# Two of the four sums of Strassen's weight blocks made by accumulating DMAs of GpSimd's queue, with signs of the combinations turned

## What is computed

```
h = rmsnorm(concat(meta_tokens, x), norm_gain)
q, k, v, f_logit, z_att, u, gate_b, gate_c, z_conv, m_att, m_conv = split(h @ w_in)
y_att  = (forgetting_attention(q, k, v, log_sigmoid(f_logit + b_f)) * silu(z_att)) @ w_att_o
y_conv = (gate_b * short_conv(gate_c * u, conv_w) * silu(z_conv)) @ w_conv_o
out    = rmsnorm(x + (sigmoid(m_att) * y_att + sigmoid(m_conv) * y_conv) @ w_out, final_gain)
```

## Time and profile before

| what | us |
|---|---|
| median of 3 runs | 1209.1 |
| lowest, highest | 1209.03, 1209.93 |
| the profiled execution, first to last instruction | 1207.9 |
| PE busy | 1196.4 (99%) |
| DVE busy | 954.6 (79%) |
| ACT busy | 651.3 (54%) |
| POOL busy | 35.3 (3%) |
| PE idle in 40 to 600 us, by the windows | 2.1 |
| DVE busy in 40 to 600 us | 518.7 of 560 |

### The profile page before, as it was taken

One profiled execution on the slowest core, in us unless ns is written; L12 is line 12 of the kernel. 1 busy time (PEld: TensorE's weight loads), 2 busy tenths in 40 slices (PEclk: granted clock), 3 DMA queues, 4 the chain that ended last, 5 costly groups with the idle time before them and its releaser, 6 DMA issues.

```text
span 1207.9 us, 18441 instructions
## 1 busy us (share of the span) xinstructions
PE 1196.4 (99%) x7252; PEld 1070.4 (89%) x7252; DVE 954.6 (79%) x1111; ACT 651.3 (54%) x868; POOL 35.3 (3%) x50
## 2 busy tenths in 40 slices
PE   9999999999999999999999999999999999999997
PEld 8998898898888988889888899999999999888886
DVE  6989988988989989999966556877787778755544
ACT  7666555556656566656555444445544554543533
POOL 1000000000000000000000010111011101000000
PEclk9999999999999999999999999999999999999999
DMA  6788898887888898898578865555655565665663
GB/s 214 241 296 274 272 296 262 276 301 257 273 288 288 272 293 287 268 310 271 192 234 267 268 188 179 157 168 163 210 155 173 154 200 169 219 212 176 213 221 123
DMA packets 181249, 280.40 MB, mean 232 GB/s; under 512 B 9296, under 2 KB 128160, under 8 KB 180768
## 3 DMA queue, kind: packets, MB, share of 16 engines
q1 hardware_dynamic: 171760, 263.49, 66.9%
q10 hardware_dynamic: 9408, 15.78, 4.2%
HBM read 270.83 MB, written 8.41 MB: 231 GB/s over the span
## 4 chain that ended last, share of the span: by engine, by line
PE 87%; DVE 10%; issue 1%; ACT 1%; DMA 0%; ACTq 0%; POOLq 0%; POOL 0%; DVEq 0%
PE ps L1481 22%; PE ps L1483 22%; PE ps L1482 22%; PE ps L1497 7%; PE ps L1496 6%; PE ps L1498 3%; PE ps L1495 3%; DVE w_lo L1052 2%; DVE w_lo L1089 2%; DVE w_lo L1086 2%; DVE quads L1068 1%; DVE quads L1070 1%; DVE quads L1066 1%; DMA chan_rows<-in_norm_gain 0%; PE ps L1506 0%
## 5 line engine op out<-in xcount | busy, mean ns | idle before, releaser
L934 DVE TENSOR_TENSOR w_lo<-w_raw,w_hi 128x1024 fp32r<-128x1024 f32 x196 | 238.6, 1235 | 97.9 <-ACT w_hi L610 96.9
L1481 PE MATMUL ps<-h,w_hi 128*128 128x258 f32 (+1 forms) x1024 | 293.6, 287 | 1.3 <-DVE w_lo L1052 1.0
L1482 PE MATMUL ps<-h,w_hi 128*128 128x258 f32 (+1 forms) x1024 | 291.2, 284 | 0.0
L1483 PE MATMUL ps<-h,w_lo 128*128 128x258 f32 (+1 forms) x1024 | 291.0, 284 | 0.0
L610 ACT CAST w_hi<-w_raw 128x1024 fp32r<-128x1024 f32 x198 | 203.8, 1050 | 112.0 <-PE ps L1483 64.2
L1481 PEld LDWEIGHTS ps<-h,w_hi 128*128 128x128 f32 x1024 | 192.7, 188 | 5.3 <-issue 1.8
L1482 PEld LDWEIGHTS ps<-h,w_hi 128*128 128x128 f32 x1024 | 192.9, 188 | 2.1
L1483 PEld LDWEIGHTS ps<-h,w_lo 128*128 128x128 f32 x1024 | 192.8, 188 | 0.0
L1052 DVE TENSOR_TENSOR w_lo<-w_raw,w_hi 128x1024 fp32r<-128x1024 f32 x122 | 148.7, 1220 | 15.9 <-ACT w_hi L666 15.7
L1497 PE MATMUL ps<-h,w_hi 128*128 128x512 f32 x408 | 159.9, 397 | 1.0 <-DVE w_lo L1052 0.9
L1496 PE MATMUL ps<-h,w_hi 128*128 128x512 f32 x360 | 142.5, 396 | 0.0
(11 more groups left out here) (213 smaller groups left out, 2085.9 us busy)
## 6 DMA issues: line engine op xcount, KB each, us to landing
w_raw<-in_w_in SPq DMA_DIRECT2D x226, 512.0 KB, 4.8
quads<-in_w_in SPq DMA_DIRECT2D x144, 512.0 KB, 4.3
w_raw<-in_w_conv_o SPq DMA_DIRECT2D x32, 512.0 KB, 5.8
w_raw<-in_w_att_o SPq DMA_DIRECT2D x32, 512.0 KB, 4.5
w_raw<-in_w_out SPq DMA_DIRECT2D x32, 512.0 KB, 4.3
quads<-in_w_in SPq DMA_DIRECT2D x48, 256.0 KB, 4.7
gates_dram<-stage ACTq DMA_DIRECT2D x24, 256.0 KB, 4.5
gate_nat<-gates_dram ACTq DMA_DIRECT2D x8, 512.0 KB, 4.5
```

The costliest lines, as they stand in the source:

```text
L934: nc.vector.tensor_tensor(w_lo[:, lo_slot(c), :], w_raw[:, c % RAW, :], w_hi[:, hi_slot(c), :].bitcast(F32), ALU.subtract).then_inc(w_spli ...
L1481: nc.tensor.matmul(dst, a_hi, b_hi, start=start, stop=False, skip_group_check=resumed)
L1482: nc.tensor.matmul(dst, a_hi, b_lo, start=False, stop=False, skip_group_check=resumed)
L1483: return nc.tensor.matmul(dst, a_lo, b_hi, start=False, stop=stop, skip_group_check=resumed)
```

## The change

The right half of row 0 of a quad, b12, gets its first sum from a DMA. GpSimd waits until the two loads of the buffer have landed (`quad_landed`) and issues a DMA of 128 by 512 floats (256 KB) from `w_in` that is added to what lies there (`accum_op=ALU.add`). In a first-half step it adds b11, in a second-half step b22, both read from HBM again. The end of this DMA is told by three new semaphores `t_added`, one for each buffer. 96 such DMAs stand in GpSimd's list, ahead of its loop for the attention stage.

DVE no longer does anything for the first-half sum, and does two sums instead of three in a second-half step. ACT's cast of the first-half sum waits for `t_added`, and so does DVE's first sum of a second-half step. The loads on SP's queue are unchanged: all four blocks are still loaded, b22 for its own product.

Since a DMA can add and not subtract, b12 now enters as b12 + b11 and b12 + b22, that is with the sign of the right block column turned. This is made good elsewhere: a sum of the frame blocks becomes a difference (line 1115 of the kernel before), and two sums of frame blocks and two of the four output blocks of each group are made by SCALAR_TENSOR_TENSOR, -1 times the first operand minus the second. These 14 instructions replace 14 TENSOR_TENSOR of the same size.

The cut diff:

```diff
     found = []
     for step, after in enumerate(STEP_AFTER):
         before = STEP_AFTER[step - 1] if step > 0 else -3
-        if step < STEPS:
-            places = [(after, 0)]
-        else:
-            spread = min(3, after - before)
-            places = [(after - spread + 1 + part * spread // 3, part) for part in range(3)]
-        found += [(g, step, part) for place, part in places if place == r]
+        if step >= STEPS:
+            spread = min(2, after - before)
+            places = [(after - spread + 1 + part * spread // 2, part) for part in range(2)]
+            found += [(g, step, part) for place, part in places if place == r]
     return found
...
-    per = STEPS + 3 * STEPS
-    return g * per + (step + 1 if step < STEPS else STEPS + 3 * (step - STEPS) + part + 1)
+    return (g * STEPS + step - STEPS) * 2 + part + 1
...
+        t_added = [sem(f"t_added{q}") for q in range(QUADS)]
...
+        def quad_added(g, step):
+            return ((g * len(STEP_AFTER) + step) // QUADS + 1) * 16
...
+
+            w_in_k = w_in.rearrange("(k p) n -> p k n", p=P)
+            for g in range(GROUPS):
+                for step in range(2 * STEPS):
+                    q, k = quad(g, step), 2 * (step % STEPS) + step // STEPS
+                    col = quad_col(g) + k % 2 * HALF
+                    pool.wait_ge(quad_landed[q], quad_fill(g, step))
+                    nc.gpsimd.dma_start(quads[:, q, 0, HALF:], w_in_k[:, k, col:col + HALF], accum_op=ALU.add
+                                        ).then_inc(t_added[q], 16)
+
             with pool.Fori(0, PAIRS) as i:
...
-                    act.wait_ge(t_made, sums_made(g, step, 0))
+                    act.wait_ge(t_added[q], quad_added(g, step))
                     act.wait_ge(w_used, slot_reused(c + 1))
                     nc.scalar.copy(w_hi[:, hi_slot(c + 1), 0:HALF], quads[:, q, 0, HALF:]).then_inc(w_rounded, 1)
                 else:
-                    act.wait_ge(t_made, sums_made(g, step, 1))
+                    act.wait_ge(t_made, sums_made(g, step, 0))
                     act.wait_ge(w_used, slot_reused(c))
                     nc.scalar.copy(w_hi[:, hi_slot(c), :], quads[:, q, 0, :]).then_inc(w_rounded, 1)
-                    act.wait_ge(t_made, sums_made(g, step, 2))
+                    act.wait_ge(t_made, sums_made(g, step, 1))
                     act.wait_ge(w_used, slot_reused(c + 1))
                     nc.scalar.copy(w_hi[:, hi_slot(c + 1), :], quads[:, q, 1, :]).then_inc(w_rounded, 1)
...
                 q = quad(g, step)
-                b11, b12, b21, b22 = (quads[:, q, k, n * HALF:(n + 1) * HALF] for k in range(2) for n in range(2))
+                b11, b12, b21 = (quads[:, q, k, n * HALF:(n + 1) * HALF] for k, n in ((0, 0), (0, 1), (1, 0)))
                 if part == 0:
-                    dve.wait_ge(quad_landed[q], quad_fill(g, step))
-                else:
-                    dve.wait_ge(t_made, sums_made(g, step, part - 1))
-                if step < STEPS:
-                    nc.vector.tensor_tensor(b12, b12, b11, ALU.subtract).then_inc(t_made, 1)
-                elif part == 0:
-                    nc.vector.tensor_tensor(b12, b22, b12, ALU.subtract).then_inc(t_made, 1)
-                elif part == 1:
+                    dve.wait_ge(t_added[q], quad_added(g, step))
                     nc.vector.tensor_tensor(b11, b12, b11, ALU.add).then_inc(t_made, 1)
                 else:
-                    nc.vector.tensor_tensor(b21, b11, b21, ALU.subtract).then_inc(t_made, 1)
+                    dve.wait_ge(t_made, sums_made(g, step, 0))
+                    nc.vector.tensor_tensor(b21, b11, b21, ALU.add).then_inc(t_made, 1)
...
                 elif n == 7:
                     dve.wait_ge(s_step, 2)
-                    nc.vector.tensor_tensor(a22, a21, a22, ALU.add).then_inc(s_made, 1)
+                    nc.vector.tensor_tensor(a22, a22, a21, ALU.subtract).then_inc(s_made, 1)
...
                 elif n == 12:
-                    nc.vector.tensor_tensor(a11, a22, a11, ALU.subtract).then_inc(s_made, 1)
+                    nc.vector.scalar_tensor_tensor(out=a11, in0=a22, scalar=-1.0, in1=a11, op0=ALU.mult,
+                                                   op1=ALU.subtract).then_inc(s_made, 1)
                 elif n == 13:
                     dve.wait_ge(s_made, 3)
                     dve.wait_ge(s_step, 4)
-                    nc.vector.tensor_tensor(a12, a12, a11, ALU.subtract).then_inc(s_made, 1)
+                    nc.vector.scalar_tensor_tensor(out=a12, in0=a12, scalar=-1.0, in1=a11, op0=ALU.mult,
+                                                   op1=ALU.subtract).then_inc(s_made, 1)
...
-                    nc.vector.tensor_tensor(stage[1][:], stage[2][:], ps[:, P5_BANK, :], ALU.add
-                                            ).then_inc(c12_made, 1)
+                    nc.vector.scalar_tensor_tensor(out=stage[1][:], in0=stage[2][:], scalar=-1.0,
+                                                   in1=ps[:, P5_BANK, :], op0=ALU.mult, op1=ALU.subtract
+                                                   ).then_inc(c12_made, 1)
                     dve.wait_ge(c12_made, g + 1)
                     nc.vector.tensor_tensor(stage[2][:], stage[2][:], ps[:, P7_BANK, :], ALU.add
                                             ).then_inc(v_made, 1)
                     dve.wait_ge(v_made, g + 1)
                     dve.wait_ge(gate_stored[C11], (g + 1) * 16)
-                    nc.vector.tensor_tensor(stage[0][:], stage[2][:], ps[:, P2_BANK, :], ALU.subtract
+                    nc.vector.tensor_tensor(stage[0][:], stage[2][:], ps[:, P2_BANK, :], ALU.add
                                             ).then_inc(c21_made, 1)
                     dve.wait_ge(c21_made, g + 1)
                     dve.wait_ge(p5_kept, g + 1)
-                    nc.vector.tensor_tensor(stage[2][:], stage[2][:], p5[:], ALU.add).then_inc(c22_made, 1)
+                    nc.vector.scalar_tensor_tensor(out=stage[2][:], in0=stage[2][:], scalar=-1.0, in1=p5[:],
+                                                   op0=ALU.mult, op1=ALU.subtract).then_inc(c22_made, 1)
```

More of the change, by code:

```diff
@@ L435, in quad_fill, with quad_col @@
             return ((g * len(STEP_AFTER) + step) // QUADS + 1) * 32
+        def quad_added(g, step):
+            return ((g * len(STEP_AFTER) + step) // QUADS + 1) * 16
+        def quad_col(g):
+            return (COL_MC, COL_MA, COL_Z)[g // 2] + g % 2 * GROUP_COLS
         def group_out(g, part):
@@ L515, in load_quad @@
                 q, k = quad(g, step), 2 * (step % STEPS)
-                col = (COL_MC, COL_MA, COL_Z)[g // 2] + g % 2 * GROUP_COLS
+                col = quad_col(g)
                 sp.dma_start(quads[:, q, 0, :], w_in_k[:, k, col:col + GROUP_COLS]).then_inc(quad_landed[q], 16)
```

## The result

The changed kernel takes 1260.1 us (median of 4 runs, 1258.1 to 1262.7) against 1209.1 (1208.7 to 1209.9, 4 runs): a ratio of 1.042, 95% interval 1.041 to 1.043. It is 51 us slower, where 2.7 us less was forecast, and lies outside the range.

A forecast was written before the change was run, and what follows sets the result against it. The prediction took PE to bound the kernel, with only its conv-stage idle time to gain. -3.2 us for relieving DVE and +0.5 for late transfers gave -2.7, so 1206.4 us, with a range of 1205.0 to 1232.

The forecast's parts named there:

- DVE's relief: Conv stage: 96 sums leave DVE, so PE's pauses behind DVE's low parts go; gain 3.2 us, from 2.1 to 3.5.
- The hidden part of a pause: PE's timeline in the conv stage: modelled matmul ends hide some 0.23 us of each pause, at six places.
- The signs: DVE's 14 SCALAR_TENSOR_TENSOR in place of TENSOR_TENSOR: claimed to take the same time, cost nothing.
- Room of 12.1 us for load and addition: Quad buffers: 12.1 us from a load's issue to the sum needing it; first halves claimed to have no less.
- My rule: Conv loop: each us of load and addition over 12.1 costs 16 us over 48 second-half steps, 32 with first halves.
- The addition takes 4.3 us: GpSimd's adding DMA: 3.6 us as a similar plain load takes, plus 0.7 for the second read.
- my upper bound of 7.2: GpSimd's adding DMA: at most two plain 256 KB transfers in a row at the median, 7.2 us.
- The loads grow by 1.2 us: Quad loads on SP's queue: queueing lengthens them by half the distance to their worst, 1.2 us, leaving 1.4 spare.
- Load on the engines: DMA engines in the conv stage: 320 GB/s of work, or 365 at double cost; claimed to fit, with 0 to 7% spare.
- my second rival: Conv stage: DMA engines saturate as additions cost double, 600 us of work in 560; 1240 us taken, chance 0.12.
- Late ones are caught by DVE's lead: Conv stage: DVE rebuilds its lead at 0.9 us a step and absorbs late additions; 0.5 us charged for the rest.
- The first rival: Conv loop: load and addition exceed 12.1 us and become the wait; 1217 us, span 1211.5 to 1230, chance 0.26.

The follow-up runs named there:

- the sixteen columns: Changed kernel with each adding DMA adding 16 columns (8 KB) in place of 512, all waits kept, rest of the first sum left out: 1207.0 us, ratio 0.9982.
- the copy: Changed kernel with GpSimd's DMA copying over the buffer's quarter instead of adding, all waits kept: 1219.4 us, ratio 1.009.
- the halved loads: Changed kernel with each conv-unit load after the first 16 bringing half its rows, additions and waits kept: 1231.6 us, ratio 1.019.
- the earlier start: Changed kernel with each adding DMA waiting only for the load of its own row, not for both loads: 1240.5 us, ratio 1.025.
- the four-buffer kernel: Changed kernel with a fourth quad buffer for the 64 steps of the first four groups, all additions and waits kept: 1236.1 us, ratio 1.022.

## Why the prediction was wrong

- **PE is the bound, and DVE's relief is worth 3.2 us.** Right in kind, and probably a little low: 1205.0 against 1209.8 without the adding DMAs, 4.7 us, with 3.5, my upper bound, still inside the interval. The hidden part of a pause was sized from one pause.
- **The signs cost nothing.** Right, shown alone. That GpSimd's next work comes after 740 us was misread, it starts at 708.75; the last addition is issued at 636.7, so nothing hangs on it.
- **Room of 12.1 us for load and addition.** Right for the middle of a second half, where it was read, and too large for its start, where the kernel before has 9.5 to 11.7 us and where 24.0 of PE's 35.4 idle us arose. It was also read as a limit for the median, and 11.5 already cost 10 us. These are whole distributions; the load alone reaches 9.7 us. My rule, a third of a us for each us over 12.1, does well once it is applied to each turn and not to the median: by my estimate from the traces it gives 5, 12, 36, 40 and 58 us for the sixteen columns, the copy, the halved loads, the earlier start and the changed kernel, and against the run without additions they lost 2, 14, 27, 35 and 56.
- **The addition takes 4.3 us.** *This is the step that failed*, the term of the sum that was mis-sized most. It takes 6.8, near my upper bound of 7.2. I took the nearest row, a plain load issued by ACT on emptier engines, and added 0.7 us for a second read by bytes. A GpSimd-issued addition of 8 KB already lands in 4.7 us, a 256 KB copy from the same queue in 5.3, and the addition adds 1.5 to that.
- **The loads grow by 1.2 us.** They grew by 1.5. Together 5.2 + 1.2 + 4.3 = 10.7 us was assumed and 13.5 measured, 1.4 over the room where I had 1.4 to spare.
- **Load on the engines.** The double cost (365 GB/s) was the true one, and the share of 0.99 to 1.04 is what my second rival needed. But the quad loads did not double (4.8 to 6.3 us), and the rival's mechanism is refuted as a cause by itself: at 1.04 and 1.03 PE did not idle when nobody waited or a fourth buffer stood by. Full engines count only through the turn: they lengthen load and addition.
- **Late ones are caught by DVE's lead.** Wrong: 0.5 us was charged for those that are not, and PE idles 35.4 us in the stage. The wait for the addition stands in front of DVE's other work (104.95 above, with two conv units' low parts behind it), and 89 of 96 turns are late.
- **The first rival** described what happened, with its signs: L1075 waits 72.0 us and L692 58.2 us for the addition. With the measured excess its own rule gives 1.4 x 32 = 45, less the relief 40 us; 51 were measured. It held no term for PE's clock: 16.4 of the 53.1 us of span are PE's extra busy time, which the lower clock around its pauses accounts for. So it is in part luck that the rule comes as near as it does. The case ended at 1230 since it was given an excess of 0.7 us; with 1.4 in both halves the rule passes 1230 without the clock.

Open: why landings stayed at 6.1 and 6.5 us with the engines at 0.93, the pauses of the four-buffer kernel in group 1, and its one late addition in group 4. No run separates how much of 4.7 us is GpSimd's building of the transfer.

## What to carry to other kernels

Before a DMA is put behind another one in the same buffer, compare the sum of both landings, near their worst and not at the median, with the time in which the buffers come round, and take that time where it is shortest, at the seams of the loop. Where it doesn't fit, one more buffer can help more than less traffic: here it took the pauses away for 200 us, while a tenth less traffic left 22 of 51 us. Price a DMA by its queue, its kind and the load that it will meet: a plain load of another queue on emptier engines said 3.6 us, and the GpSimd-issued addition took 6.8. And ask what stands behind a new wait in its engine's order: here data that had long landed was held up behind it, and the tensor engine paid twice, by the pause and by the clock after it.

## What the runs showed of the hardware

- An accumulating DMA from HBM to SBUF takes the engines 2.0 times as long as a copy of the same bytes (2340 against 1149 us for 25.17 MB), and GpSimd 0.86 us to issue where a copy took 0.55.
- Between shares of 0.93 and 1.04 its landing changed little, 6.5 and 6.8 us. Emptier engines no run shows.
- A share of 1.04 at 328 GB/s for 270 us did not hold up a three-buffer ring that only loads.
- A tensor_tensor of 128x512 on GpSimd takes 1.69 us beside a busy DVE, and DVE's sums and low parts with two SBUF inputs grow, from 1.22 to between 1.29 and 1.53 us and from 0.69 to between 0.87 and 0.99.
- After a pause of TensorE of 4.4 us its granted clock was 0.61 and 0.73 in the next two windows of 2.7 and 2.4 us, and a 512-column matmul took 0.43 us for 0.23.
